# Prompt attention of a decoder step: two narrow heads per unit, and the compressed branch of all heads in one softmax

## The reference, cut to what matters

```python
# q_nsa (1,256,2 kv,8 group,64); kv_nsa -> kv_cmp, kv_sel, kv_win, each (1,256,2,2 kv,64)
kvc = _compress(kv_cmp, cmp_w1, cmp_w2, cmp_pe)            # 15 compressed blocks
o_cmp, p_cmp = _cmp_attend(q_nsa, kvc, pos)                # softmax over the blocks that ended
o_sel = _sel_attend(...)                                   # 256 tokens: every block is selected, so plain causal
o_win = _window_prompt(q_nsa, kv_win)                      # window 512 > 256: plain causal as well
o_nsa = g[0] * o_cmp + g[1] * o_sel + g[2] * o_win         # sigmoid gates per token and head
o_dil = _dilated_mix(...)                                  # 4 outputs of width 128, from 12 heads in 3 groups
y_a = o_nsa.reshape(1, 256, 1024) @ w_br_nsa               # 16 heads x 64
y_b = o_dil.reshape(1, 256, 512) @ w_br_dil
```

## Time and profile before

| | |
|---|---|
| median of 3 runs | 2056.83 us (2054.75 to 2066.18) |
| the profiled execution | 2057.16 us, span 2055.4 us |
| TensorE busy over the span | 1928.4 us (94%) |
| DVE, ACT busy | 976.2 us (47%), 772.6 us (38%) |
| moved by the 16 DMA engines | 512.54 MB, mean 249 GB/s |
| prompt attention | about 564 to 744 us from the span's start |

### The profile page before, as it was taken

How to read it: one execution, slowest core, us unless ns; L and a number is a source line. 1 busy time by engine, 2 the same in 40 slices (tenths; PEclk the granted TensorE clock), 3 DMA queues, 4 the chain that set the end, 5 groups by cost and what they waited for, 6 DMA issues and landing times.

```text
span 2055.4 us, 36811 instructions
## 1 busy us (share of the span) xinstructions
PE 1928.4 (94%) x15765; PEld 1769.5 (86%) x15765; DVE 976.2 (47%) x1730; ACT 772.6 (38%) x1232; POOL 58.5 (3%) x108
## 2 busy tenths in 40 slices
PE   6988899999999987899999996999999999999997
PEld 4656899999955555699999996999999999999996
DVE  3336336554366642255454756344444444654544
ACT  2336333333344443243333434333333333533332
POOL 0000000000000000000000000000000000000000
PEclk9999999999999998899999998999999999999999
DMA  9997379999897755877787873777677776456551
GB/s 373 422 422 262 115 229 294 282 290 285 273 408 306 304 194 221 283 239 232 239 264 235 286 256 137 243 247 260 234 258 245 246 264 215 138 172 190 173 180 59
DMA packets 336139, 512.54 MB, mean 249 GB/s; under 512 B 8754, under 2 KB 310106, under 8 KB 319498
## 3 DMA queue, kind: packets, MB, share of 16 engines
q1 hardware_dynamic: 316146, 368.53, 54.0%
q0 software_dynamic: 5248, 125.73, 15.6%
q10 hardware_dynamic: 14640, 16.80, 2.5%
HBM read 504.29 MB, written 98.91 MB: 293 GB/s over the span
## 4 chain that ended last, share of the span: by engine, by line
PE 85%; DMA 6%; DVE 5%; ACT 2%; issue 1%; SPq 0%; DVEq 0%; ACTq 0%
PE bank L1132 18%; PE bank L1133 18%; PE bank L1134 18%; PE bank L845 5%; PE bank L846 5%; PE bank L847 5%; DMA piece<-in_w_ada 4%; PE bank L735 3%; PE bank L772 2%; PE bank L903 1%; ACT mem L1454 1%; DMA mem<-in_cache_sel_kv,runs 1%; PE bank L761 1%; PE bank L800 1%; DMA mem<-in_x_sample 1%
## 5 line engine op out<-in xcount | busy, mean ns | idle before, releaser
L1132 PE MATMUL bank<-piece,piece 128*128 128x264 f32 x3072 | 878.0, 286 | 31.4 <-DVE piece L2054 26.5
L1133 PE MATMUL bank<-piece,piece 128*128 128x264 f32 x3072 | 877.5, 286 | 0.0
L1134 PE MATMUL bank<-piece,piece 128*128 128x264 f32 x3072 | 877.0, 285 | 0.0
L2059 DVE TENSOR_TENSOR piece<-piece,piece 128x2048 fp32r<-128x2048 f32 (+2 forms) x216 | 441.1, 2053 | 483.0 <-ACT piece L1544 483.0
L1132 PEld LDWEIGHTS bank<-piece,piece 128*128 128x128 f32 x3072 | 582.9, 190 | 32.3 <-issue 22.7
L1544 ACT CAST piece<-piece 128x2048 fp32r<-128x2048 f32 (+2 forms) x216 | 369.0, 1715 | 569.4 <-PE bank L1134 531.1
L1134 PEld LDWEIGHTS bank<-piece,piece 128*128 128x128 f32 x3072 | 582.9, 190 | 0.0
L1133 PEld LDWEIGHTS bank<-piece,piece 128*128 128x128 f32 x3072 | 582.3, 190 | 0.0
L845 PE MATMUL bank<-piece,piece 128*128 128x264 f32 (+1 forms) x816 | 240.1, 294 | 0.0
L846 PE MATMUL bank<-piece,piece 128*128 128x264 f32 (+1 forms) x816 | 234.0, 287 | 0.0
L847 PE MATMUL bank<-piece,piece 128*128 128x264 f32 (+1 forms) x816 | 233.6, 286 | 0.0
(11 more groups left out here) (324 smaller groups left out, 1416.6 us busy)
## 6 DMA issues: line engine op xcount, KB each, us to landing
piece<-in_w_ada SPq DMA_DIRECT2D x48, 2048.0 KB, 12.7
out_s_dil<-in_cache_dil_kv POOLq DMA_DIRECT2D x64, 1023.5 KB, 6.3
piece<-in_w_in SPq DMA_DIRECT2D x50, 1024.0 KB, 8.2
piece<-in_w_gate SPq DMA_DIRECT2D x22, 2048.0 KB, 8.1
piece<-in_w_up SPq DMA_DIRECT2D x22, 2048.0 KB, 8.1
piece<-in_w_down SPq DMA_DIRECT2D x32, 1408.0 KB, 6.6
piece<-in_w_in SPq DMA_DIRECT2D x16, 2048.0 KB, 8.9
piece<-in_w_out SPq DMA_DIRECT2D x8, 2048.0 KB, 8.5
```

What stands on the lines that cost most here:

```text
L1132: mm(out, w_high[:, k, :], half_tile(x_high[k]), start=(start and k == first_tile), stop=False)
L1133: mm(out, w_high[:, k, :], half_tile(x_low[k]), start=False, stop=False)
L1134: last = mm(out, w_low[:, k, :], half_tile(x_high[k]), start=False, stop=(stop and k == len(x_high) - 1))
L2059: v.tensor_tensor(half_chunk(a, k_tiles, f, CW), raw, half_chunk(buffer, k_tiles).bitcast(F32), ALU.subtract)\
```

## The change

- The narrow units become 16: unit ("n", qt, g) handles head g of both key/value groups. The scores of group 0 and group 1 come from the upper and the lower 64 rows of the array (their queries and keys lie on partitions 0 to 63 and 64 to 127) and go to banks 0 and 1. Four masked maxima of W columns, four exponentials, four scalings; 8 or 4 transposes; the values of group 0 go to partitions 0 to 63 of the output and those of group 1 to 64 to 127, their matmuls alternating.
- The compressed branch leaves the units. `cmp_scores` takes all 32 score products (16 heads, 2 query tiles, 15 columns each) in turn 0, `compressed(0)` and `compressed(2)` on DVE and one exponential over 480 columns on ACT (unit 1) make one softmax of them, `cmp_turns` (turns 3 and 4) transposes it, ACT copies it in four pieces. In `pv` one matmul with 30 rows of probabilities and a block-diagonal value matrix (30 x 128) stands for both heads. For that the prompt's compressed values are made twice, with zeros beside them.
- The 24 steps of `ada` go one to a turn, turns 0 to 22, with two in turn 1 (`UNIT_OF_STEP`). The wait of SP for `select(9)` moves from behind the load of step 8 to behind that of step 12. The row buffer is single.
- `select` keeps unit 9 and goes on in units 13 to 19.
- `oN` holds head g of both groups in one tile, so `w_br_nsa` is loaded in two transfers of 64 partitions each in place of one of 128, and the sample's result is copied into `oN` in two pieces in place of four.

```diff
-    UNITS = [("d", qt, h) for h in range(HG) for qt in range(QT)] + [("n", qt, h) for h in range(H) for qt in range(QT)]
+    UNITS = [("d", qt, h) for h in range(HG) for qt in range(QT)] + [("n", qt, g) for g in range(G) for qt in range(QT)]
-    STEP_AT = {1 + i * (NU - 2) // NF: NA1 + i for i in range(NF)}
-    PART_END = {1 + (ADA_STEPS * (i + 1) - 1) * (NU - 2) // NF: ADA_FIRST + i for i in range(NF // ADA_STEPS)}
+    UNIT_OF_STEP = {NA1 + i: i if i < 2 else i - 1 for i in range(NF)}
+    PART_END = {UNIT_OF_STEP[(p + 1) * ADA_STEPS - 1]: p for p in range(ADA_FIRST, ADA_PARTS)}
...
+            if a == NA1 + 12:
...
+                for kv in range(KVH):
+                    sp.dma_start(slot(2)[kv * DH:(kv + 1) * DH, 0:8, :], head_rows(kv, slice(0, CW))).then_inc(w_ld["merge"][2], 16)
...
+                for base in (0, DH):
+                    for h in range(2):
+                        last = mm(bank[6][base:base + 2 * NBP, P + h * DH:P + (h + 1) * DH], pgv[0:64, 2 * NBP * h:2 * NBP * (h + 1)],
+                                  w2[0:64, 1, :], start=True, stop=True)
...
                 for br in range(2):
-                    mm(bank[0][:, br * W:(br + 1) * W], q, kT[r, br + 1, 0:W], start=True, stop=True)
-                mm(bank[1][:, 0:NBP], q, kcP[r, 0:NBP], start=True, stop=True).then_inc(*pe_.mark("s", u))
+                    for kv in range(KVH):
+                        r = slice(kv * DH, (kv + 1) * DH)
+                        last = mm(bank[kv][:, br * W:(br + 1) * W], qK[r, h, qt * P:(qt + 1) * P], kT[r, br + 1, 0:W], start=True, stop=True)
+                last.then_inc(*pe_.mark("s", u))
...
-                last = mm(out, v, PT[0:k, n * P:(n + 1) * P], start=(n == 0), stop=(n == len(bl) - 1))
+            if kind == "n":
+                r = slice(h % 2 * DH, h % 2 * DH + 2 * NBP)
+                mm(out, vcP[r, :], cmp_pt[r, qt, h // 2 * P:(h // 2 + 1) * P], start=True, stop=False)
+                half = len(bl) // 2
+                for n in range(half):
+                    for kv in range(KVH):
+                        t = kv * half + n
+                        last = mm(out[kv * DH:(kv + 1) * DH, :], bl[t][1], PT[t // 4][:, t % 4 * P:(t % 4 + 1) * P],
+                                  start=False, stop=(n == half - 1))
...
+        def cmp_scores():
+
+            for qt in range(QT):
+                for g in range(G):
+                    for kv in range(KVH):
+                        r, x = slice(kv * DH, (kv + 1) * DH), qt * G + g
+                        last = mm(bank[7 - 2 * kv][:, x * NBP:(x + 1) * NBP], qK[r, g, qt * P:(qt + 1) * P], kcP[r, 0:NBP], start=True, stop=True)
+            last.then_inc(*pe_.mark("cmp_s"))
+
+        def cmp_turns(qt):
+
+            pe.wait_ge(*(act_.at("cmp_pt", 0) if qt else dve_.at("cmp_p")))
+            for g in range(G):
+                last = mm(bank[7][g % 2 * DH:g % 2 * DH + 2 * NBP, g // 2 * P:(g // 2 + 1) * P],
+                          cmp_p[:, qt, 2 * g:2 * g + 2, :].rearrange("p x n -> p (x n)"), ident, start=True, stop=True)
+            last.then_inc(*pe_.mark("cmp_t", qt))
...
-            if u in STEP_AT:
-                ada(STEP_AT[u])
+                cmp_scores()
+            for a, at_unit in UNIT_OF_STEP.items():
+                if at_unit == u:
+                    ada(a)
+            if u in (3, 4):
+                cmp_turns(u - 3)
+            if u == ND:
+                pe.wait_ge(*act_.at("cmp_pt", 1))
             if 1 <= u <= NU:
                 probs(u - 1)
...
+            if u in TURN_AT:
+                if TURN_AT[u] == ADA_FIRST + 1:
...
+            for c in range(0, tiles_, 4):
+                w = min(4, tiles_ - c) * P
+                cp(PT[c // 4][:, 0:w], bank[2 + c // 4][:, 0:w]).then_inc(*act_.mark(*(("pt", u) if c + 4 >= tiles_ else ())))
 
...
                 e = E[:, u % 2, :]
                 if kind == "n":
-                    for br in range(3):
-                        a, z = (br * W, (br + 1) * W) if br < 2 else (2 * W, 2 * W + NBP)
-                        A(e[:, a:z], e[:, a:z], ACT.Exp, bias=small[:, 8 * (u % 2) + br:8 * (u % 2) + br + 1], scale=SC_N,
-                          accum_out=small[:, 16 + 8 * (u % 2) + br:17 + 8 * (u % 2) + br])\
-                            .then_inc(*act_.mark(*(("e", u) if br == 2 else ())))
+                    for x in range(2 * KVH):
+                        a, z = x * W, (x + 1) * W
+                        A(e[:, a:z], e[:, a:z], ACT.Exp, bias=small[:, 8 * (u % 2) + x:8 * (u % 2) + x + 1], scale=SC_N,
...
                 o_copy(u - 2)
-            if u == 19:
+            if u == 1:
+                act.wait_ge(*dve_.at("cmp_m"))
+                A(cmp_p, cmp_p, ACT.Exp, scale=SC_N).then_inc(*act_.mark("cmp_e"))
+            if u in (3, 4):
+                act.wait_ge(*pe_.at("cmp_t", u - 3))
+                for base in (0, DH):
...
-                    act.dma_start(slot(2)[:, 0:8, :], rows(w_bn, bass.ds(i * CW, CW))).then_inc(w_ld["merge"][2], 16)
+                    for kv in range(KVH):
+                        act.dma_start(slot(2)[kv * DH:(kv + 1) * DH, 0:8, :], head_rows(kv, bass.ds(i * CW, CW))).then_inc(w_ld["merge"][2], 16)
...
+        def compressed(u):
+            if u == 0:
+                dve.wait_ge(*cmp_stored.at("p_cmp"))
+                dve.wait_ge(*pe_.at("cmp_s"))
+                for kv in range(KVH):
+                    v.tensor_tensor(cmp_p[:, :, kv:H:KVH, :], bank[7 - 2 * kv][:, 0:QT * G * NBP].rearrange("p (q x n) -> p q x n", q=QT, n=NBP),
+                                    over_tokens("cmp_add", G), ALU.add).then_inc(*dve_.mark())
+                dve.wait_ge(*dve_.last())
+                link(v.tensor_reduce(cmp_stat, cmp_p, AX.X, ALU.max))
+                v.tensor_tensor(cmp_p, cmp_p, over_blocks(cmp_stat), ALU.subtract).then_inc(*dve_.mark("cmp_m"))
+            if u == 2:
+                dve.wait_ge(*act_.at("cmp_e"))
+                link(v.tensor_tensor(cmp_p, cmp_p, over_tokens("cmp_mul"), ALU.mult))
+                link(v.tensor_reduce(cmp_stat, cmp_p, AX.X, ALU.add))
+                link(v.tensor_scalar(cmp_stat, cmp_stat, 1e-30, None, ALU.max))
+                link(v.reciprocal(cmp_stat, cmp_stat))
+                for kv in range(KVH):
+                    v.tensor_tensor(cmp_stat[:, :, kv:H:KVH], cmp_stat[:, :, kv:H:KVH], gates[:, :, kv * G:(kv + 1) * G], ALU.mult)\
+                        .then_inc(*dve_.mark())
+                dve.wait_ge(*dve_.last())
+                v.tensor_tensor(cmp_p, cmp_p, over_blocks(cmp_stat), ALU.mult).then_inc(*dve_.mark("cmp_p"))
...
-                    v.tensor_tensor_reduce(e[:, br * W:(br + 1) * W], bank[0][:, br * W:(br + 1) * W], mask, 1.0, -3e38,
-                                           ALU.add, ALU.max, mx[:, br:br + 1]).then_inc(*dve_.mark())
-                v.tensor_tensor_reduce(e[:, 2 * W:2 * W + NBP], bank[1][:, 0:NBP], const("cmp_add")[:, qt * NBP:(qt + 1) * NBP],
...
+                    v.tensor_tensor_reduce(e[:, x * W:(x + 1) * W], bank[x // 2][:, x % 2 * W:(x % 2 + 1) * W], mask, 1.0, -3e38,
+                                           ALU.add, ALU.max, mx[:, x:x + 1]).then_inc(*dve_.mark(*(("max", u) if x == 2 * KVH - 1 else ())))
                 dve.wait_ge(*dve_.last())
...
-                                            const("cmp_mul")[:, qt * NBP:(qt + 1) * NBP], 1.0, 0.0, ALU.mult, ALU.add,
-                                            den[:, 2:3]))
                 link(v.tensor_scalar(den, den, 1e-30, None, ALU.max))
...
-                v.tensor_tensor(den[:, 0:2], den[:, 0:2], g3[:, 1:3], ALU.mult).then_inc(*dve_.mark())
-                link(v.tensor_tensor(den[:, 2:3], den[:, 2:3], g3[:, 0:1], ALU.mult))
-                for br in range(3):
-                    a, z = (br * W, (br + 1) * W) if br < 2 else (2 * W, 2 * W + NBP)
-                    v.tensor_scalar(e[:, a:z], e[:, a:z], den[:, br:br + 1], None, ALU.mult)\
-                        .then_inc(*dve_.mark(*(("p", u) if br == 2 else ())))
+                g4 = gates[:, qt, :].rearrange("p (r kv g) -> p kv r g", r=3, kv=KVH)[:, :, 1:3, h]
+                link(v.tensor_tensor(den.rearrange("p (kv r) -> p kv r", kv=KVH), den.rearrange("p (kv r) -> p kv r", kv=KVH), g4, ALU.mult))
+                for x in range(2 * KVH):
+                    v.tensor_scalar(e[:, x * W:(x + 1) * W], e[:, x * W:(x + 1) * W], den[:, x:x + 1], None, ALU.mult)\
+                        .then_inc(*dve_.mark(*(("p", u) if x == 2 * KVH - 1 else ())))
             else:
```

More of the change, by code:

```diff
@@ L745, in ada_turn @@
             for f in range(4):
-                last = turn(ada_banks(part_)[1][:, f * P:(f + 1) * P], ada_row[:, part_ % 2, f * P:(f + 1) * P], ident)
+                last = turn(ada_banks(part_)[1][:, f * P:(f + 1) * P], ada_row[:, f * P:(f + 1) * P], ident)
             last.then_inc(*pe_.mark("ada_turn", part_))
@@ L830, in _ @@
```

(36 more changed lines are left out.)

116 lines of the change are left out of this document (54 added, 62 removed).

## The result

The changed kernel takes 2033.99 us (median of 4 runs, 2029.48 to 2036.51), against 2059.15 for the kernel before on the same chip: ratio 0.9872, 95% interval 0.9837 to 0.9907, some 25 us less. Its profiled execution has a span of 2031.3 us. The forecast was 2034.

The account below looks back on a forecast made before the run. TensorE, the DVE-ACT loop and the w_ada stream were taken as nearly equal bounds. Units from 617.5 reach 705.0, drain 711.5, gather 716.5, TensorE 721 against 744: 23 us less, 2034, range 2022 to 2047.

Parts of the forecast that it names:

- Start of the narrow units: Prompt's attention: the w_ada stream, 5.0 us a piece, delays DVE's first narrow unit to 612.5 from 594.3, 18 us later.
- next bound, 606.5: Before the narrow units: 8 dilated units of 3.7 us and 12.4 for the compressed branch end by 606.5.
- The compressed branch at 0: Turn 0 on: its added work is covered by the wait for the stream; 0, up to 5 as a bound.
- The loop: Narrow units on DVE and ACT: 5.5 us for tile 1, 4.2 for tile 0, 9.7 a pair.
- SP's wait and the gather: Turn 12: constants and gather ahead of load 13 delay step 13 to 640, unit 13 to 645; some 5 us.
- What TensorE takes from the loop: Narrow units: turns with TensorE late and the slow clock cost 4.7 us, half of 9.3; bounds 0 and 19.
- The rest at 0: Merge's additional load issues cost 0; added value matmuls and fewer copies are each under 1 us.
- (a): Narrow units' scores: row halves work one after the other, 3.4 us a pair, total 2042; chance 0.17.
- (b): Prompt's attention: less is lost, the gather yields and TensorE keeps up, 31 us less, 2025; chance 0.17.
- (c): Prompt's attention: the w_ada stream becomes the bound throughout, no change, 2055; chance 0.08.
- (d): Narrow pairs: waits for loads leave TensorE at 1.2 GHz, 19.6 us a pair, slower at 2089; chance 0.05.
- The value matmuls: Narrow pair on TensorE: column halves run side by side, values 2.3 us; the skill's rule would give 3.9.

Follow-up runs that it names:

- e1: Changed kernel with 1 MB in place of 2 MB loads for the second half of w_ada, same instructions: 2024.97 us, ratio 0.9829.
- e14: The changed kernel itself, run again for comparison on the same chip as the four-edit version: 2033.52 us, ratio 0.9871.
- e6: Changed kernel without VectorE's passes over the compressed scores after their first mask: 2036.03 us, ratio 0.9872.
- e12: Changed kernel with the prompt's compressed branch left out altogether: 2031.66 us, ratio 0.9875.
- e13: Changed kernel with 1 MB loads for the second half of w_ada and the prompt's compressed branch left out: 2018.93 us, ratio 0.9803.
- e3: Changed kernel with the sample's first gather also waiting for ada step 18: 2032.55 us, ratio 0.9851.
- e11: Changed kernel with first gather waiting for step 18, SP's wait two loads later, no floor on sums, last modulation turn one turn earlier: 2022.45 us, ratio 0.9821.
- e5: Changed kernel with both groups' score products taken from the same 64 rows of the array: 2041.68 us, ratio 0.9891.
- e9: Kernel before with the compressed branch left out of the narrow units: 2033.99 us, ratio 0.9869.
- e7: Changed kernel without the VectorE instruction that keeps the narrow units' sums above 1e-30: 2033.48 us, ratio 0.9857.

## Why the prediction was right, and where it was right by luck

**Start of the narrow units.** 612.5 forecast, 612.63 measured; unit 9 at 617.5, measured 617.07. The stream does hold this start back (e1), but not step by step as the forecast had it. It does so early, at step 2 (4.04 us of wait and a slow step); from there to step 9 TensorE works without waiting for a load, and its turns of 4.85 happen to be nearly as long as a piece's 5.0. (In e14 the waits lie before steps 2, 3 and 4, 0.86, 1.69 and 0.27, and the units start just as late.) The prediction's next bound, 606.5, was met as well (606.29 in e1), and that was luck: it added 12.4 for the compressed branch, which costs 4.5, and nothing for the four additional steps, which cost 7.7.

**The compressed branch at 0.** Right, with the cover that was named: e6 (passes) and e12 (all of it) move the start by 0.6 at most. Its price without the cover was put at up to 12 us; e1 against e13 gives 4.5 to 5.4. The 64 product instructions were put at 7.7 us and take 3.75, since here too the halves run in pairs; the passes at 4.7 take 5.0.

**The loop.** Forecast 5.5 and 4.2, together 9.7; measured 10.0 between two places without a choice of blocks, and units 13 to 23 take 65.5 us (647.16 to 712.7), just what the forecast's terms give for them: eleven units 54.0, seven choices 11.15, one folding 0.35.

**SP's wait and the gather.** Sample's queries 625.3 forecast, 624.9 measured; step 13 at 640, measured 639.47; unit 13 at 645, measured 647.16. The two that are missing are the low clock: step 13 takes 3.64 in place of 1.9, and the transposes behind it 1.82. (From 639.2 to 645 the prediction's figures give 5.8, and its sum carries "some 5".) e3 confirms that the gather's bytes are the larger part.

**What TensorE takes from the loop: the term that failed.** The forecast set 4.7 us for turns in which TensorE is late inside the loop, as half of a remainder of the kernel before. In the changed kernel the chain has no such turn from unit 13 on; the term measures 0. In its place stand 2.2 us at unit 13, which is the low clock, 2.6 in the drain (9.1 from 712.7 to 721.84, against 6.5), and the 0.5 or so that the sum had rounded away: 5.3 in all. Of the drain's 2.6 about half is the clock. The other half is work that the prediction left out: the last turn of the modulation and its folding stand behind the last values, 1.65 us from 720.19 to 721.84, where the drain before ended in a copy of 0.27. In e11, where that turn comes one turn earlier, the drain takes 6.94 (705.04 to 711.98). The sum, 721 against 721.84, came out through one wrong term and unseen ones of like size. TensorE is not far off, however: 1.3 us more a pair (e5) do cost 2 us in these units.

**The rest at 0, and the rivals.** The merge kept its 264 us, and the 22.4 us of the stage's end are the gain (the span is 24.1 less, 1.7 of it behind this stage). (a) is out by e5's row, (b) and (c) by the stage's end at 722 (half of (b) came true, TensorE keeps up, but the gather didn't yield), (d) by the clock: 0.93 in the first and third window, 0.84 where step 13 waits. Of the signs that were named, one was off: the DMA share stays near 1.00 up to 645, not 620.

**What the prediction did not say.** It told the sum of two parts, not their shares, and its own terms held them: the 18 us lost at the start are about what the pairing gains in the loop (17 from e9 to e12). Only e9 and e12 show that nearly the whole net gain is the compressed branch leaving the units, with the late start as the cover for its one softmax.

**The value matmuls.** The prediction took column halves to run side by side, by rows of another stage, against the rule of the Trainium skill ("TensorE: Matmul & The Clock Gate", Part 3, What overlaps and what doesn't) that a weight load overlaps a running matmul only where row groups differ. The trace decides against the rule for this case: both halves use all 128 rows, and 16 instructions take 1.09 us; at the 0.138 of the kernel before they would take 2.2. No run takes the two halves away from the value matmuls, as e5 does for the scores, so this rests on the two kernels' rows.

## What to carry to other kernels

A small operand that goes through every step of a softmax on its own costs by the instruction, not by its columns: 15 columns a unit took 1.4 us of a 7.6 us pair, 23 us in all, and nearly nothing once all of them were handled at once under a wait for the stream. Fewer and longer turns move whatever was spread over them: count the background steps and loads per turn, and see whether the stream can still follow. Where two changes come together, take each out by itself before praising either, and look at what stands in the stream ahead of a load that a turn waits for.

## What the hardware showed that I had not expected

The longer waits for a load were each followed by a step at the lower clock: 3.64 after 4.04 us (577.68) and after 6.98 (639.47), 3.41 after 4.70 (e1). Of the waits between 2.2 and 2.8 us some were (3.34 after 2.78 in e3, 3.19 after 2.29 in e11), and two were not (1.92 after 2.33, at 578.45 in e7 and at 569.76 in e12); those of 0.49 and 0.46 were not. So the length of the wait alone doesn't decide it; what does stays open. Some steps ran slow with no wait for a load just before them (3.52 at 688.91). A wait so costs its length and, behind it, up to another 1.7 us in the first step.

A few us in which TensorE has little to do at the end of a stage (1.14 us busy in 4.7) nearly double the price of the drain's instructions: eight transposes 1.76 us, in e11 1.09; sixteen value instructions 1.98 where they had taken 1.09 ten us before. The drain of the kernel before was not free of it: its last ten value instructions took 2.60 us (741.28) against 1.38.
